# Block 2's norms: the squares of the chunks added on VectorE, one product with the ones

## The reference

```
def rms_norm(x, g):
    return x * lax.rsqrt(jnp.mean(x * x, axis=-1, keepdims=True) + EPS) * g

for l in range(2):
    hn = rms_norm(h, norm_mix_g[l])
    q, k, v, xr, gate = split(hn @ w_in[l])
    ...                                            # attention and recurrent branch
    h = h + concatenate([o_attn, o_rec]) @ w_out[l]
    hn = rms_norm(h, norm_ffn_g[l])
    g, u = split(hn @ w_gu[l])
    h = h + (silu(g) * u) @ w_down[l]
```

## Time and profile before

| | |
|---|---|
| three runs | 2007.71, 2011.70, 2017.32 us |
| median | 2011.7 us |
| profiled execution, span from first to last instruction | 2007.7 us |
| PE busy | 1935.9 us, 96% of the span |
| PE weight load busy | 1182.1 us, 59% |
| VectorE busy | 634.2 us, 32% |
| ScalarE busy | 403.6 us, 20% |
| GpSimd busy | 730.4 us, 36% |
| moved by DMA | 553.94 MB |

### The profile page before, as it was taken

One profiled execution on the slowest core, in us unless ns is written; L12 is line 12 of the kernel. 1 busy time (PEld: TensorE's weight loads), 2 busy tenths in 40 slices (PEclk: granted clock), 3 DMA queues, 4 the chain that ended last, 5 costly groups with the idle time before them and its releaser, 6 DMA issues.

```text
span 2007.7 us, 27189 instructions
## 1 busy us (share of the span) xinstructions
PE 1935.9 (96%) x9937; PEld 1182.1 (59%) x9938; DVE 634.2 (32%) x1337; ACT 403.6 (20%) x975; POOL 730.4 (36%) x401
## 2 busy tenths in 40 slices
PE   7999989999999999999999998999999999999999
PEld 5788743333333333333333334877888888788887
DVE  1573642323323232333232223473101016520100
ACT  1222432222122121221122123252000012510000
POOL 0000027777776777777767773000000000000000
PEclk8989989999999999999999999999999999999999
DMA  9793579999999999999999999432443552344430
GB/s 309 220 306 127 208 300 385 416 418 418 417 419 387 417 419 417 417 419 417 417 398 410 418 419 346 154 127 84 139 123 87 177 185 80 120 152 130 116 101 21
DMA packets 245904, 553.94 MB, mean 276 GB/s; under 512 B 16560, under 2 KB 178722, under 8 KB 212946
## 3 DMA queue, kind: packets, MB, share of 16 engines
q1 hardware_dynamic: 236336, 547.96, 72.5%
q10 hardware_dynamic: 8946, 3.87, 0.8%
q0 software_dynamic: 560, 1.25, 0.3%
HBM read 551.98 MB, written 1.06 MB: 275 GB/s over the span
## 4 chain that ended last, share of the span: by engine, by line
PE 63%; DMA 23%; POOL 6%; DVE 4%; issue 1%; ACT 1%; SPq 0%; POOLq 0%; ACTq 0%; DVEq 0%
PE bank L1825 17%; DMA ring_and_columns<-in_w_up_dram 13%; PE bank L1553 8%; PE bank L2057 8%; POOL ring_and_columns L1491 6%; DMA ring_and_columns<-in_w_down_dram 5%; PE bank L1574 4%; PE bank L1830 4%; PE bank L1152 4%; DMA anteroom_last<-in_w_up_dram 3%; DMA anteroom_last<-in_w_down_dram 3%; PE bank L1840 2%; PE bank L1411 1%; PE bank L1946 1%; PE bank L1158 1%
## 5 line engine op out<-in xcount | busy, mean ns | idle before, releaser
L1491 POOL COPY ring_and_columns<-ring_and_columns 128x2048 f32<-128x2048 f32 x298 | 575.4, 1936 | 267.4 <-PE bank L1553 119.5
L1553 PE MATMUL bank<-ring_and_columns,x_expert 128*64 128x512 f32 x2176 | 480.0, 596 | 7.5 <-POOL ring_and_columns L1491 7.5
L1553 PEld LDWEIGHTS bank<-ring_and_columns,x_expert 128*64 128x64 f32 x2176 | 152.2, 137 | 332.9 <-issue 291.0
L1825 PE MATMUL bank<-ring_and_columns 128*128 128x272 f32 (+1 forms) x1536 | 342.4, 386 | 0.0
L1825 PEld LDWEIGHTS bank<-ring_and_columns 128*128 128x128 f32 x1536 | 291.8, 190 | 49.9
L1574 PE MATMUL bank<-ring_and_columns,act_t_e 128*64 128x512 f32 x1088 | 242.4, 598 | 6.8 <-DVE act_t_e L1674 6.8
L1574 PEld LDWEIGHTS bank<-ring_and_columns,act_t_e 128*64 128x64 f32 x1088 | 77.8, 137 | 149.5 <-issue 142.5
L2057 PE MATMUL bank<-ffn_act,ring_and_columns 128*128 128x272 f32 (+1 forms) x704 | 158.1, 386 | 0.0
L1491 POOL COPY ring_and_columns<-anteroom_last 128x2048 f32<-128x2048 f32 x74 | 143.6, 1941 | 38.2 <-DMA anteroom_last<-in_w_up_dram 19.6
L2057 PEld LDWEIGHTS bank<-ffn_act,ring_and_columns 128*128 128x128 f32 x704 | 133.7, 190 | 22.8
L1666 DVE TENSOR_SCALAR pass_work<-bank 128x512 f32<-128x512 f32 x34 | 23.5, 691 | 374.3 <-PE bank L1553 374.3
(11 more groups left out here) (504 smaller groups left out, 1820.2 us busy)
## 6 DMA issues: line engine op xcount, KB each, us to landing
ring_and_columns<-in_w_up_dram SPq DMA_DIRECT2D x207, 1024.0 KB, 10.1
ring_and_columns<-in_w_down_dram SPq DMA_DIRECT2D x103, 1024.0 KB, 10.3
anteroom_last<-in_w_up_dram SPq DMA_DIRECT2D x49, 1024.0 KB, 10.1
ring_and_columns<-in_w_gu_dram SPq DMA_DIRECT2D x44, 1024.0 KB, 5.6
ring_and_columns<-in_w_in_dram SPq DMA_DIRECT2D x33, 1024.0 KB, 10.7
anteroom_last<-in_w_down_dram SPq DMA_DIRECT2D x25, 1024.0 KB, 10.3
ring_and_columns<-in_w_ada_dram SPq DMA_DIRECT2D x24, 1024.0 KB, 10.9
ring_and_columns<-in_w_down_dram SPq DMA_DIRECT2D x32, 704.0 KB, 5.9
```

Of the source, the lines that this page charges most:

```text
L1491: pool.tensor_copy(ring[:, j, :], waiting_tile(g)).then_inc(ante_copied, 1)
L1553: ins = mm(bank[CAP * half:CAP * half + CAP, :], xe[:, k, :], ring[:, k, a:a + 512], start=False, stop=(k == CHUNKS - 1))
L1825: ins = mm(bank[:, 0:columns], w[:, k, P * m:P * m + P], src[:, k, 0:columns], start=(k == 0), stop=(k == CHUNKS - 1))
```

## The change

VectorE adds the squares of the chunks into chunk 0's tile, `sq[:, 0]`, as they come. PE makes a single product of the ones with that sum for each norm, in place of eight.

- `mean_part` becomes `over_partitions`: one product, started and stopped by itself. It waits for a new semaphore count, `n_total` or `f_total`, which VectorE raises with its last addition.
- Mixing norm of layer 0: VectorE makes the seven additions behind its tables, each waiting for ACT's square. PE's single product stands behind the x loop.
- FFN norms: VectorE makes the addition behind each square. PE's single product stands behind the first of the 44 gate/up groups, no longer ahead of them. Ahead of that group PE now waits for `out2_added` 2, since the old products, which covered the reading of bank 0, are gone.
- Mixing norm of layer 1: VectorE makes the addition behind each square. In the down loop of layer 0 PE waits for `down_added` from chunk 6 on, where a bank comes up a second time.
- The squares of VectorE now count on its own steps; `f_sq` is gone.

```
-            def mean_part(bank, k, n, sem, count, done):
+            def over_partitions(bank, n, sem, count, done):
                 pe.wait_ge(*at(sem, count))
-                ins = mm(pb[bank][:, 0:n], ones[:], sq[:, k, 0:n], start=(k == 0), stop=(k == CHUNKS - 1), skip_group_check=True)
-                if k == CHUNKS - 1:
-                    ins.then_inc(t2[done], 1)
+                mm(pb[bank][:, 0:n], ones[:], sq[:, 0, 0:n], start=True, stop=True).then_inc(t2[done], 1)
...
-                    if l == 0 and k:
-                        mean_part(4, k - 1, T2, "n_sq", k, "n_summed")
-                mean_part(4, CHUNKS - 1, T2, "n_sq", 8 * l + 8, "n_summed")
+                over_partitions(4, T2, "n_total", l + 1, "n_summed")
...
-                    mean_part(3, m - 4, n, "f_sq", 8 * l + m - 3, "f_summed")
-                for k in range(4, CHUNKS):
-                    mean_part(3, k, n, "f_sq", 8 * l + k + 1, "f_summed")
...
+                    if j == 0:
+                        pe.wait_ge(*at("out2_added", 8 * l + 2))
...
+                            if j + r + m == 0:
+                                over_partitions(3, n, "f_total", l + 1, "f_summed")
...
                 for m in range(CHUNKS):
+                    if l == 0 and m >= 6:
+                        pe.wait_ge(*at("down_added", m - 4))
...
-                    if l == 0 and m >= 1:
-                        mean_part(4, m - 1, T2, "n_sq", 8 + m, "n_summed")
...
+            def add_square(k, n, total):
+
+                ins = tt(sq[:, 0, 0:n], sq[:, 0, 0:n], sq[:, k, 0:n], ALU.add)
+                if k == CHUNKS - 1:
+                    ins.then_inc(t2[total], 1)
+                else:
+                    st(ins)
...
+                if l == 0:
+                    dve.wait_ge(*at("n_sq", 1))
+                    for k in range(1, CHUNKS):
+                        dve.wait_ge(*at("n_sq", k + 1))
+                        add_square(k, T2, "n_total")
...
-                    tt(sq[:, m, 0:n], x, x, ALU.mult).then_inc(t2["f_sq"], 1)
+                    st(tt(sq[:, m, 0:n], x, x, ALU.mult))
+                    if m:
+                        add_square(m, n, "f_total")
...
-                        tt(sq[:, m, :], x, x, ALU.mult).then_inc(t2["n_sq"], 1)
+                        st(tt(sq[:, m, :], x, x, ALU.mult))
+                        if m:
+                            add_square(m, T2, "n_total")
```

More of the change, by code:

```diff
@@ L221 @@
     "o2_root": ("ym_ready", 4), "o2_rows": ("cmp_scored", 1), "o2_turned": ("cmp_logit", 1), "att_ready": ("cmp_exp", 1),
-    "out2_made": ("cmp_prob", 1), "out2_added": ("cmp_turned", 1), "f_sq": ("cmp_pt", 1), "f_summed": ("ya_ready", 4),
+    "out2_made": ("cmp_prob", 1), "out2_added": ("cmp_turned", 1), "f_summed": ("ya_ready", 4),
     "f_root": ("y_made", 4), "f_h": ("yg_turned", 4), "gu_made": ("yg_made", 5), "g_sig": ("y_root", 2),
@@ L225 @@
     "x_out": ("x1_turned", 4), "rows_out": ("n2_summed", 1), "stored": ("xr_in", 16), "steps2": None, "steps2_a": None,
+    "n_total": ("routed", 1), "f_total": ("den_made", 1),
 }
```

## The result

The changed kernel took 1998.41 us (median of 5 runs, 1997.38 to 2002.11), the kernel before 2012.45 us (median of 5, 2007.71 to 2017.32): a ratio of 0.9932, 95% interval 0.9910 to 0.9953. A second series on another occasion gave 2001.26 us (6 runs) against 2011.78 us (11 runs): 0.9937, interval 0.9914 to 0.9959. (The ratios are estimates from the runs, not the quotients of the two medians.) Forecast were 1999.0 us and 12.6 us less; the medians moved by 14.0 and 10.5 us, and a single median carries a stretch of low clock described at the end. The profiled execution took 1996.5 us from first to last instruction, 11.2 us less than before: block 2 is 12.8 us shorter, but what stands ahead of it, which the change does not touch, took 1.6 us more (block 2 begins at 1242.62 in place of 1241.01 us).

The account below looks back on a forecast made before the run. PE was taken to bound block 2, with room on VectorE and ACT. Removing 28 products (9.62 + 3.02 = 12.64 us), additions hidden, gave 2007.7 - 12.6 = 1995.1 us, or 1999.0 from the median 2011.7; range 1991 to 2008.

Parts of the forecast that it names:

- all four places: Block 2's mixing and FFN norms in both layers: PE sets the time; 28 products leave, together 12.64 us.
- The price of a product: Products with the ones in PE's chain: 0.458 us at 272 columns, 0.432 at 256, not the mean record duration.
- The first norm: Layer 0's mixing norm, behind a PE pause: seven products leave, 3.2 us; room for the sum 8.1 us.
- the slow piece: 16 records behind PE's 4.1 us pause before the first norm, 5.59 us instead of 3.67; said to stay as it is.
- rival 3: PE's stream gains 1 to 3 us beyond the products (fewer operand switches, fewer waits): 1997 us; chance 5%.
- The loss that the forecast drew from the rule: VectorE's additions: by the skill's rule the change is worth about nothing if they stood in PE's way.
- The tight place: FFN norms: sum ready at T + 1.6 us, PE asks at T + 3.67; room 2.0 us, in layer 1 1.9.
- T: End of the last output product before an FFN norm, 1391.15 us in the trace before the change.
- Rival 1: VectorE's sums arrive last, PE stands before each single product: +8.4 us, 2020 us, slower; chance 4%.
- upper bound: VectorE addition step of 0.95 us, should the in-place operand cost a second pass; last FFN sum still in time.
- Rival 2: First norm's stretch set by VectorE and ACT's chunks; 3.2 us stay hidden, 2002.3 us; chance 6% with other small losses.

Follow-up runs that it names:

- fillers: Changed kernel plus nine products of the ones with a constant table in PE's 4.1 us pause ahead of the first norm; x loop stage 15.36 us.
- product first: Changed kernel with the FFN norms' single product back ahead of the first gate/up group; 1.83 and 1.77 us more in the two stages.
- four more: Changed kernel with four further VectorE additions ahead of each of the seven in the FFN norms; 3.55 us more in layer 0, 5.58 in layer 1.
- two more: Changed kernel with two further VectorE additions ahead of each of the seven in the FFN norms; stages unchanged, 182.23 and 171.64 us.
- recurrent norm's edit: Changed kernel with the recurrent norm's four products made one, VectorE adding the squares; layer 1 attention stage 82.49 against 82.95 us.
- additions only: Kernel before with all 32 products, plus the 28 VectorE additions into a tile that nobody reads; block 2 took 772.5 us.
- after again: Changed kernel once more, timed beside the kernel before and two further versions; 2001.26 us, ratio to before 0.9937.

## Why the prediction was right

- What bounds it. PE's stream set the time in all four places: each stage shrank by the products taken out, and no wait grew. (The slices of the page before are less even than the text ahead of the prediction says: in block 2 VectorE's digits run from 0 to 7, and one of PE's is 8. The forecast used the stages, so nothing hangs on it.)
- The time. That 1999.0 us forecast and 1998.41 us measured lie so close is in part luck. The forecast took 12.6 us from a median of three, 2011.7 us; the median of five was 2012.45 us, and the two series moved by 14.0 and 10.5 us. What was forecast well is the 12.85 us of the stages.
- The price of a product. 0.458 and 0.432 us, from the chain. Three of the stages gave 3.21, 3.21 and 3.02 us against 3.21, 3.21 and 3.02. Had the mean duration of two records been taken (0.78 and 0.76 us), the sum would have been 22 us.
- The first norm gave 3.41 in place of 3.21 us. The forecast said that the slow piece stays as it is; it does not, to a fraction of a us: this stage read 16.8 to 18.4 us over the profiles with the same loop and no fillers, with the length of its half-clock piece. The 0.2 us is within that, so neither it nor a gain of the stream beyond its products (rival 3) is shown.
- The additions. 442 and 425 ns (28 of them, 0.9 us idle), a step of 0.47 us, 3.30 us for seven; forecast 0.48. The size that the forecast took from the Trainium skill's "VectorE: DVE Perf Modes" (441 ns) holds here. Its rule in "The DRAIN you can't avoid" holds for these additions, each of which needs the one before; the eight products of L2467, which wait for nothing between them, took 3.39 us at 0.50 us each, so there the next one starts before the last one ends. The loss that the forecast drew from the rule did not come, since VectorE's time was free.
- The tight place. Sum at T + 1.66 (forecast 1.6), asked for at T + 3.67, yT at T + 10.1 (forecast 10). That the new place gives the room was shown by product first (in the old place 3.6 us of the 12.85 are lost) and by four more.
- Rival 1 is real, but the point from which it decides was put too late. The forecast named 1.15 us a step from the last chunk's three steps alone, and let VectorE catch up at 0.95 us. It left out the backlog of the chunks before: from the second chunk's start (1371.75 us) VectorE has 21 steps to make until PE asks (1391.65 us), so if every step grows alike it decides at 19.9 / 21 = 0.95 us (an estimate), which was the forecast's upper bound. By the same count four more additions a chunk, 49 steps of 0.476 us, bring the sum at T + 7.1 us; it came at T + 7.05. With two more it came at T + 2.61, in time. The step of 0.47 us is half of what would decide.
- Rival 2 fell: the first norm's gain came whole, 3.41 us.
- What the forecast had not seen is why single times differ by 5 us: it put the spread down to runs, and the trace before held no half-clock stretch in its attention part.

## What to carry to other kernels

Price an instruction in a pipelined stream by the distance to the next one in the chain, not by its duration. Work moved to a second engine is free as long as the result is ready when the first engine asks; compute that time for each place from the arrival of its inputs, and if it is tight, move the question later (here behind one group of products) before making the answer faster. When two runs of one design differ by more than the edit, compare stages, and compare the granted clock of each.

## What the runs showed of the hardware

The attention part, the same instructions in nearly all kernels, took 85.73 or 90.4 us in layer 0 and 82.95 or 87.6 us in layer 1 (84.5 to 89.3 and 82.5 to 86.6 are the versions with the recurrent norm's edit; 84.5 is 89.3 less the 4.7 us, not measured). In the longer ones the granted clock is 0.50 for some 10 us. PE was not idle for long before it: the waits there are 0.8 us at most in kernels with and without the stretch. In the run with additions only the clock fell at about 1351.8 us. From 1344 to 1348 us PE was 3.21 of 4.00 us busy there, with products of 16 output rows (L1968) and then small ones of mostly 128 columns, from 1348 to 1352 us 4.00 of 4.00. The kernel before did the same 2.9 us earlier, and its clock stayed at 1.00. First the run with additions only, then the kernel before:

```profile
1344.00:1348.00 4.00, 3.21 (x31) 1.62 (x29) 3.68 (x17) 3.58 (x13) 0.00 (x0) 1.00 0.10 22
```

```profile
1341.00:1345.00 4.00, 3.21 (x29) 1.59 (x27) 3.68 (x19) 3.45 (x13) 0.00 (x0) 1.00 0.11 22
1345.00:1349.00 4.00, 4.00 (x32) 2.84 (x32) 3.99 (x13) 1.38 (x7) 0.00 (x0) 1.00 1.06 350
```

So what PE did there does not alone decide whether the clock falls.

The Trainium skill's "TensorE: Matmul & The Clock Gate", "HAM oscillation", ties a falling clock to pauses of PE. That agrees with the first norm (a pause of 4.1 us, and full clock with fillers in it); no such pause stands ahead of the stretch in the attention part. What releases it there was not found: of ten profiles with the attention part unedited four show it in layer 0, one in layer 1 and five nowhere. The changed kernel has a profile with it and one without; so has the kernel before, if the run with additions only is counted to it.

Pauses of about the same length went either way too. With four more additions PE paused for 1.44 and 1.57 us in layer 0's FFN norm and kept a clock of 1.00; in layer 1's it paused for 1.85 and 1.51 us, with one product between, and the clock was 0.50 behind them.

The mean granted clock of the runs goes with their times. Beside "after again", the kernel before took 2009.2 to 2012.3 us in seven runs with a clock of 0.982 to 0.984, and 2016.0 to 2019.1 in four with 0.978 to 0.981; the changed kernel 1995.9 to 1998.2 in three of 0.982 to 0.984, and 2004.4 to 2005.1 in three of 0.978 to 0.980. The medians of the groups differ by 13.1 and 12.7 us, close to the 12.8 us of the stages. The groups were made with the times known. The changed kernel's six runs fall into two halves, so its median of 2001.26 us lies between them, where no run is; that is why the medians differ by 10.5 us only.
